# A two-block network on one core: the second head pair's key is taken before its decays, its projections' first terms move to ScalarE, gate slices move, and each attention group's last pair is placed behind a dense tile

## The reference

```python
proj = h @ w_in[l]
att_in, rwkv_in, gate_in = jnp.split(proj, [ATT_IN, ATT_IN + RWKV_IN], axis=-1)
y_att = attention_mixer(att_in) @ w_att_out[l]          # 3 groups x 8 heads of 64, blocks of 128
y_rwkv = rwkv7_mixer(rwkv_in, mu_shift[l], w0[l], ...) @ w_rwkv_out[l]
...
# rwkv7_mixer: z is mixed with the token before, then r, k, v and three low-rank inputs
z = z + (z_prev - z) * mu
w_log = -jax.nn.softplus(-(w0 + jnp.tanh(w_low) @ w2)) - 0.5
decay = jnp.exp(-jnp.exp(w_log))
a = jax.nn.sigmoid(a0 + a_low @ a2)
k_mod = k * (1.0 + (a - 1.0) * k_a)
kk = heads(k * k_k)
kk = kk / jnp.maximum(jnp.sqrt(jnp.sum(kk * kk, axis=-1, keepdims=True)), 1e-12)
# a scan over tokens, 16 heads of 64: state = state*w + (state@(-kk))*(kk*a) + v*k_mod ; y = state@r
bonus = jnp.sum(r_h * k_h * r_k, axis=-1, keepdims=True) * v_h
```

## Time and profile before

| | us |
|---|---|
| median of 3 runs | 2147.8 (2145.29 to 2149.35) |
| the profiled execution, its own time | 2148.11 |
| its span | 2146.1 |
| PE busy | 2053.9 (96%) |
| DVE busy | 1208.1 (56%) |
| POOL busy | 1062.3 (49%) |
| ACT busy | 518.1 (24%) |
| mean granted TensorE clock | 0.979 |

### The profile page before, as it was taken

The page is one execution under the profiler, slowest core; times in us unless marked ns, Lnnn a source line. Parts: engine busy times, 40 slices in busy tenths (PEclk is TensorE's granted clock), DMA queues, the critical chain, the costliest instruction groups (busy, mean ns, idle before and its releaser), DMA issues.

```text
span 2146.1 us, 39153 instructions
## 1 busy us (share of the span) xinstructions
PE 2053.9 (96%) x16093; PEld 1680.8 (78%) x16093; DVE 1208.1 (56%) x1560; ACT 518.1 (24%) x1110; POOL 1062.3 (49%) x776
## 2 busy tenths in 40 slices
PE   8999999899999998999997999999999989999998
PEld 6888787778777787788875877888876868888887
DVE  6888714466667653301178577667772646565423
ACT  2100002333334221303232122232122113232201
POOL 6777664434434464354453033222353665666663
PEclk9999999899999998999998999999999999999999
DMA  4323332253444331221322121112112422223231
GB/s 139 100 89 98 108 98 61 69 163 118 156 124 127 118 98 60 79 75 63 111 54 80 33 63 44 34 55 64 43 51 76 165 97 79 98 98 98 93 102 60
DMA packets 180342, 189.98 MB, mean 89 GB/s; under 512 B 8141, under 2 KB 161372, under 8 KB 179932
## 3 DMA queue, kind: packets, MB, share of 16 engines
q1 hardware_dynamic: 172288, 181.81, 26.6%
q10 hardware_dynamic: 7900, 5.94, 0.9%
HBM read 179.30 MB, written 8.44 MB: 87 GB/s over the span
## 4 chain that ended last, share of the span: by engine, by line
PE 55%; DVE 9%; DVEq 1%; ACT 1%; issue 1%; DMA 1%; ACTq 0%
PE bank L831 8%; PE bank L832 8%; PE bank L833 8%; PE bank L1463 7%; PE bank L1561 2%; PE bank L1424 1%; PE bank L1300 1%; PE bank L1302 1%; PE bank L1301 1%; PE bank L1284 1%; PE bank L1208 1%; PE bank L1209 1%; PE bank L1210 1%; DVE sq L2593 1%; PE bank L966 1%
## 5 line engine op out<-in xcount | busy, mean ns | idle before, releaser
L678 POOL TENSOR_TENSOR wlo<-raws,whi 128x1024 fp32r<-128x1024 f32 (+5 forms) x312 | 675.6, 2165 | 46.5 <-issue 1.5
L676 POOL TENSOR_SCALAR whi<-raws 128x1024 fp32r<-128x1024 f32 (+5 forms) x312 | 333.4, 1069 | 631.7 <-PE bank L1302 259.6
L831 PE MATMUL bank<-hbuf,whi 128*128 128x512 f32 (+2 forms) x840 | 329.1, 392 | 0.0
L833 PE MATMUL bank<-hbuf,wlo 128*128 128x512 f32 (+2 forms) x840 | 327.4, 390 | 0.0
L832 PE MATMUL bank<-hbuf,whi 128*128 128x512 f32 (+2 forms) x776 | 302.6, 390 | 0.0
L628 POOL TENSOR_TENSOR spare<-ones 1x1 f32<-1x1 f32 x92 | 22.5, 244 | 361.8 <-PE bank L833 246.2
L831 PEld LDWEIGHTS bank<-hbuf,whi 128*128 128x128 f32 (+2 forms) x840 | 157.0, 187 | 35.7 <-POOL wlo L678 1.1
L833 PEld LDWEIGHTS bank<-hbuf,wlo 128*128 128x128 f32 (+2 forms) x840 | 157.0, 187 | 34.1
L832 PEld LDWEIGHTS bank<-hbuf,whi 128*128 128x128 f32 (+2 forms) x776 | 145.1, 187 | 31.2
L2488 DVE TENSOR_REDUCE nmax<-bank 128x4 f32<-128x512 f32 (+3 forms) x40 | 21.1, 550 | 151.9 <-PE bank L1183 104.2
L1300 PE MATMUL bank<-hbuf,whi 128*128 128x512 f32 x192 | 84.1, 438 | 0.0
(11 more groups left out here) (482 smaller groups left out, 4612.2 us busy)
## 6 DMA issues: line engine op xcount, KB each, us to landing
adaw<-in_w_ada SPq DMA_DIRECT2D x64, 384.0 KB, 4.0
raws<-in_w_up SPq DMA_DIRECT2D x22, 1024.0 KB, 4.9
raws<-in_w_in SPq DMA_DIRECT2D x41, 512.0 KB, 4.0
raws<-in_w_in SPq DMA_DIRECT2D x18, 1024.0 KB, 5.0
raws<-in_pool_w_in SPq DMA_DIRECT2D x16, 1024.0 KB, 5.3
raws<-in_mla_w_in SPq DMA_DIRECT2D x10, 1024.0 KB, 6.2
raws<-in_pool_w_out SPq DMA_DIRECT2D x8, 1024.0 KB, 4.9
raws<-in_mla_w_out SPq DMA_DIRECT2D x8, 1024.0 KB, 5.2
```

Source lines behind the costliest of these rows:

```text
L676: G.tensor_scalar(h_, r_, 1.0, 1.0, ALU.mult, ALU.mult)
L678: G.tensor_tensor(l_, r_, f32(h_), ALU.subtract).then_inc(raw_split, 1)
L831: M.matmul(dst, wh, acts[k][0], start=(first and k == 0), stop=False)
L833: mm = M.matmul(dst, wl, acts[k][0], start=False, stop=(last and k == n - 1))
```

## The change

Four edits:

1. **Attention.** In the last pair of every group, `following(0)` (24 dense matmuls) stands ahead of both `turned` and of the `values` of the pair before, not between them. The product goes to bank 2 (its sequel to 3), since banks 0 and 1 still hold scores; ACT's query copies and the low-rank products swap banks with it.
2. **Pair 1's key and first terms.** `columns_of(1)` runs at the start. After the bonus product of pair 0, ACT makes the first term (the bank times 1 - mu) of pair 1's k, r and v, with a Copy from PSUM with scale, in place of three DVE TENSOR_SCALARs. DVE takes the key before `log_decays(1)`, and ACT squares it before `decays(1)`. `key_lengths(1)` stays behind the decays.
3. **`bonus_sums(0)`** stands ahead of the last four of the 24 projection slices of pair 1, and ACT copies pair 0's first gate ahead of `decays(0)`.
4. **Gate slices.** Pair 1's 48 gate matmuls stand behind steps 3, 6 and 15 of the first preparation.

```diff
-GATES_BESIDE = {6: (0, 24), 12: (24, 27), 14: (27, 30), 16: (30, 33), 17: (33, 36), 19: (36, 39), 20: (39, 42),
-                21: (42, 45), 23: (45, 48)}
+GATES_BESIDE = {3: (0, 20), 6: (20, 34), 15: (34, 48)}
...
-                        if kind or (g and j):
+                        if kind:
                             two_tiles("att", sg + kind * 2 + j, j, 3 * g + kind, h_out)
+                        elif g and j:
+                            for b in range(2):
+                                bank_free("att", b, 3 * g)
+                                product(bank[b][:, :], 1, 256, b * P, P, h_out, strip=None if b else sg + 1)\
+                                    .then_inc(products_done, 1)
...
                 for t in range(len(units) // 2):
+                    if 2 * t + 2 == len(units):
+                        following(0)
                     turned(2 * t)
                     if t == 0:
                         values_taken((0, 1))
                         scores(2)
                     else:
                         values(t - 1)
-                    if 2 * t + 2 == len(units):
-                        following(0)
                     turned(2 * t + 1)
...
                 rkv(16, 20)
                 if q >= 2:
                     gate(q - 2, q)
+                else:
+                    bonus_sums(0)
                 rkv(20, 24)
                 if q == 1:
-                    bonus_sums(0)
                     key_norms(1)
...
+            def first_term(z, out_):
+
+                product_ready(STRIP0["rkv"] + 3 + z // 2, (1, 0, 1)[z])
+                A.activation(out_[:, :], bank[z][:, :], ACT.Copy, scale=pcol[1][:, 11 + z:12 + z])\
+                    .then_inc(sem(f"rk.first{z}"), 1)
...
             key_squares(0)
             key_lengths(0)
+            take_gate(0, 0)
             decays(0)
-            take_gates(0)
-            wide_part(1)
+            take_gate(0, 1)
+            act.wait_ge(sem("rk.bon"), 1)
+            first_term(1, Kr)
+            sigmoids(1)
+            load_lora(2)
+            act.wait_ge(sem("rk.bs"), 1)
+            first_term(0, Rr)
+            first_term(2, vT[1])
+            key_squares(1)
+            decays(1)
+            key_lengths(1)
             take_gates(1)
...
                 product_ready(STRIP0["rkv"] + q * 3 + z // 2, (1, 0, 1)[z])
-                shifted(bank[z], pc[:, z:z + 1], pc[:, 11 + z:12 + z], out_[:, :]).then_inc(evac[z], 1)
+                if q == 1:
+                    dve.wait_ge(sem(f"rk.first{z}"), 1)
+                    V.scalar_tensor_tensor(out_[:, 1:S], bank[z][:, 0:S - 1], pc[:, z:z + 1], out_[:, 1:S],
+                                           ALU.mult, ALU.add).then_inc(evac[z], 1)
+                else:
+                    shifted(bank[z], pc[:, z:z + 1], pc[:, 11 + z:12 + z], out_[:, :]).then_inc(evac[z], 1)
...
-                if more:
+                if q == 1:
+                    take_key(1)
+                    log_decays(1)
+                elif more:
                     columns_of(q)
                     log_decays(q)
                     take_key(q)
```

More of the change, by code:

```diff
@@ L1244, in following @@
                     if g + 1 < ATT_GROUPS:
-                        bank_free("att", j, 3 * g + 3)
-                        product(bank[j][:, :], 0, 256, j * P, P, h_out, strip=sg + 6 if j == 0 else None)\
+                        bank_free("att", 2 + j, 3 * g + 3)
+                        product(bank[2 + j][:, :], 0, 256, j * P, P, h_out, strip=sg + 6 if j == 0 else None)\
                             .then_inc(products_done, 1)
                     elif j == 0:
-                        bank_free("lora", 0, 0)
-                        product(bank[0][:, :], 0, P, 0, P, h_out, half_at=1, strip=STRIP0["lora"])\
+                        bank_free("lora", 2, 0)
+                        product(bank[2][:, :], 0, P, 0, P, h_out, half_at=1, strip=STRIP0["lora"])\
                             .then_inc(products_done, 1)
                 for t in range(len(units) // 2):
+                    if 2 * t + 2 == len(units):
+                        following(0)
                     turned(2 * t)
@@ L1269, in _ @@
                 units_before += len(units)
-            bank_free("lora", 2, 0)
-            product(bank[2][:, :], 1, 160, 0, P, h_out, strip=STRIP0["lora"] + 1).then_inc(products_done, 1)
+            bank_free("lora", 0, 0)
+            product(bank[0][:, :], 1, 160, 0, P, h_out, strip=STRIP0["lora"] + 1).then_inc(products_done, 1)
             bank_free("lora", 3, 0)
@@ L1905, in _ @@
                         product_ready(sg + kind * 2 + t // 2, t % 2)
-                        o, x = tile(dst, t), bank[t][:, :]
+                        b = (t + 2) % 4 if g and kind == 0 else t
+                        o, x = tile(dst, t), bank[b][:, :]
                         if g:
@@ L1909, in _ @@
                         A.activation(o, x, ACT.Copy, scale=ATT_DIM ** -0.5 if kind == 0 else 1.0)\
-                            .then_inc(evac[t], 1)
+                            .then_inc(evac[b], 1)
                 units = att_units(g)
@@ L1991, in _ @@
                 if pr == 0:
-                    act.wait_ge(evac[0], fill("lora", 0) + 1)
+                    act.wait_ge(evac[2], fill("lora", 2) + 1)
                     A.activation(wlow[0:64, :], wlow[0:64, :], ACT.Tanh).then_inc(sem("lora.act"), 1)
                 if pr == 1:
-                    for b in (2, 3):
+                    for b in (0, 3):
                         act.wait_ge(evac[b], fill("lora", b) + 1)
@@ L2069, in wide_part, with take_gate @@
                     key_lengths(q)
-            def take_gates(q):
-                for turn, j in enumerate(GATE_ORDER[min(q, 1)]):
-                    if turn == 0:
-                        if q < 2:
-                            act.wait_ge(sem("x_kept"), 16)
-                        else:
-                            act.wait_ge(sem("gt.kept"), (q - 1) * 16)
-                    product_ready(STRIP0["rkv"] + q * 3 + 2, turn)
-                    A.copy(tile(xT, q % 2 * 2 + j), gate_dst(q, j)[:, :]).then_inc(sem("gt.taken"), 1)
+            def take_gate(q, turn):
+                j = GATE_ORDER[min(q, 1)][turn]
+                if turn == 0:
+                    if q < 2:
+                        act.wait_ge(sem("x_kept"), 16)
+                    else:
+                        act.wait_ge(sem("gt.kept"), (q - 1) * 16)
+                product_ready(STRIP0["rkv"] + q * 3 + 2, turn)
+                A.copy(tile(xT, q % 2 * 2 + j), gate_dst(q, j)[:, :]).then_inc(sem("gt.taken"), 1)
+            def take_gates(q):
+                take_gate(q, 0)
+                take_gate(q, 1)
+            def first_term(z, out_):
+                product_ready(STRIP0["rkv"] + 3 + z // 2, (1, 0, 1)[z])
+                A.activation(out_[:, :], bank[z][:, :], ACT.Copy, scale=pcol[1][:, 11 + z:12 + z])\
+                    .then_inc(sem(f"rk.first{z}"), 1)
             def chain(p):
@@ L2538, in _ @@
             mu = VEC0["mu_shift_2"]
-            for n, (b, half, out_, rows) in enumerate(((0, (0, 1), wlow[:, :], P), (2, (1, 0), tile(glow, 0), P),
+            for n, (b, half, out_, rows) in enumerate(((2, (0, 1), wlow[:, :], P), (0, (1, 0), tile(glow, 0), P),
                                                        (3, (1, 1), glow[0:32, S:2 * S], 32))):
@@ L2726, in _ @@
             columns_of(0)
+            columns_of(1)
             take_key(0)
```

1 line of the change is left out of this document (added).

## The result

The change is faster by nearly twice what was forecast. The median of four runs is 2128.16 us (2127.84 to 2128.3), that of before, run beside it, 2146.55 us (2144.21 to 2149.35): ratio 0.9922, 95% interval 0.991 to 0.9934, or 18.4 us between the medians where 10.35 were expected. The profiled run of after took 2127.84 us, with a span of 2126.1 us and a mean clock of 0.980.

What follows compares the result with a forecast made beforehand. PE, busy 96% of the span, was taken as the bound, so only its waits and lowered clock counted. Attention 4.15 plus RWKV start 6.2 made 10.35 us off 2147.8: 2137.45, said as 2137.5 (chance 0.55), range 2132.5 to 2142.

Steps and rivals of the forecast that it cites:

- Attention: End of each attention group: PE's three waits for exponentials (1.13, 1.51, 1.51 us) go; gain 4.15 us.
- The statistics: Softmax statistics: first send 4.0 us later, DVE's stretch shrinks from 8 to about 3.2 us, no wait at the combination.
- Rival 2: Softmax statistics arrive late, PE and DVE stand at the combination; gain only 6.1 us, 2141.5 us; chance 0.15.
- rival 3: Nearly nothing left: gates eat the gain, stall 3.8 us, decays end later, statistics late; 2.2 us, 2145.5; chance 0.09.
- rival 4: Slower: the statistics' trip through DRAM gets much longer, ending 14.4 us later; 2152 us and more; chance 0.04.
- Rival 1: More won: no POOL stall of decayed_keys, clock stays before level 6, shorter decays up to 1.5 us; 2133; chance 0.17.
- r out of bank 0 at 1159.5: RWKV start: DVE frees r at 1159.5, so gram A starts then, not at 1166.20: 6.7 us earlier.
- the move of `bonus_sums(0)`: Pair 1's projections: PE waits about 3 us for the bonus product, which costs nothing.
- The first terms: Pair 1's first terms on ACT: one TENSOR_SCALAR (0.8 us) less on DVE's path to r.
- The key ahead of the decays: Pair 1's key: its three operations, 2.1 us, leave DVE's path behind the decays to r.
- The gates: First preparation: 20 gates add 4.7 us ahead of level 0 (1168.0); fewer later, chain starts 1200.1, not 1206.33.
- The stall of `decayed_keys`: Ahead of level 6: POOL's strip split stalls DVE's decayed_keys by 1.5 us, between 0 and 3.8; PE waits 4.0 us.

Runs made afterwards that it cites:

- e1: The kernel before with the attention edit alone: 2139.25 us, ratio 0.9977.
- e7: The change with bonus_sums(0) back at its old place, behind the last projection slices: 2134.91 us, ratio 0.9951.
- e8: e7, with POOL's split of pair 2's first strip held until pair 1's decays are done: 2128.03 us, ratio 0.9919.
- e5: The change once more, nothing altered, run on another occasion: 2128.32 us, ratio 0.9919.
- e2: The change without the attention edit: 2137.48 us, ratio 0.9965.
- e12: The change with the first terms of pair 1's k, r and v made by DVE again: 2127.2 us, ratio 0.9914.
- e15: The change with ACT's squares of the key moved ahead of v's first term: 2127.15 us, ratio 0.991.
- e13: The change with DVE taking pair 1's key behind its decays again: 2135.56 us, ratio 0.9955.
- e9: The change with POOL's splits of pair 2 held, first strip until pair 1's decays, second until decayed_keys(1), are done: 2125.48 us, ratio 0.9902.
- e11: The kernel before with only POOL's split of pair 2's first strip held until pair 1's decays are done: 2142.49 us, ratio 0.9985.
- e10: e9 with the gates split 14, 14 and 20 behind steps 3, 6 and 15: 2123.9 us, ratio 0.9892.
- e14: e10 with the first terms of k, r and v on DVE again: 2122.55 us, ratio 0.9888.

## Why the prediction was wrong

The direction and the order of events were right; the size was not. The times below are put in the frame of before by adding 3.2 us, the difference between the two combinations' starts.

**Attention: right, slightly too small.** All three waits went; from the attention's start to the combination the trace is 4.8 us shorter, 4.15 were predicted, and alone (e1) it is 5.4 us by medians. What is over the sum of the three brackets stays unexplained. The statistics came nearly as told: the first send behind the dense product (1077.50), then 4.1 us of DVE work, where some 3.2 were told, and no wait at the combination. Rivals 2 and 3, which stood on their being late, fell, and rival 4, a much longer trip, with them. Rival 1 pointed the right way and was too small by 5 us: its main reason, no stall in `decayed_keys`, did not come true, and it gave shorter decays 1.5 us at most. (Rival 2's sum gives 2141.7, not 2141.5, which changes nothing.)

**The step that failed: "r out of bank 0 at 1159.5".** It held that `gram A` would wait 5 to 6 us for r and start at 1159.5, with the clock low. It was built on POOL's second strip starting "some 0.5 us later", with the decays 0.8 us earlier. In that frame the decays began at 1151.4, 1.0 later than told, but POOL began at 1153.8 and not near 1151.1. It was released by the last projection, and that came late by the bonus product's own 0.9 us and by what I left out: I priced the move of `bonus_sums(0)` as a wait of 3 us "which costs nothing", and did not let the clock fall behind it. It fell, the bonus matmuls took 2.08 us and not 1.02, and the projections behind them 0.63 us each at first and not 0.40. So POOL missed the scan, the decays took 4.3 us, where I had kept nearly the 8.4 of before, r was out at 1156.9, and `gram A` ran at 1157.1 without a wait. Two consequences: 2.4 us in its start, and about 1.7 us because the grams ran at the upper clock. Level 0 came at 1163.9 where 1168.0 was told. e7 and e8 show it: without the moved sums 6.6 us are lost, and with POOL held nothing is. How much it is varies: in e5, where the clock came back later, level 0 came 1.0 us later behind the bonus sums. The bounds given (1 us later, 2.5 us earlier) held the decays to what a shift of POOL by half a microsecond could do.

**A cost that was a gain.** The move of the bonus sums acted as an unintended hold on POOL. That is a fragile gain: without the attention part (e2) the clock stayed up and POOL met the decays again, though PE waited equally long. Why the clock stayed up there no run shows.

**The first terms: a part with no worth.** The prediction counted 0.8 us for r's TENSOR_SCALAR. e12 has all three back on DVE and is no slower. What they save on DVE is spent in ACT's queue; e15 takes one of its waits away, and the wait only moves on to r.

**The key ahead of the decays: right.** Its price was 2.1 us of DVE; undone, it costs 2.5 to 4.3 us of the length (e13 against e5 and the change), and behind its longer wait the clock is low.

**The gates: right in kind.** From level 0 to the chain the prediction has 32.1 us, the trace 31.4 (e5 32.2). The stall of `decayed_keys` was taken as 1.5 us: it is (e9 removes it and gets 1.5 us back from the wait). The wait before level 6 was told as 4.0 and was 3.84. What the prediction did not see is that the table is worth 6 us only when r is early, and that its 20 gates ahead of level 0 also cover the stall that POOL now gives `inv_U`.

**What is left.** 10.35 us foretold, 4.8 more up to the chain, 0.65 more in the attention make 15.8 of 18.4. By e5's trace it would be 1.9 less. The two spans are 20.0 us apart: the profiled run of after is 1.6 us late where the attention starts, and wins 5.8 us behind the chain's start, in code that is the same. PE of before, in the last preparation:

```profile
1597.92 0.33 PE L1463 MATMUL bank<-inv_D,inv_DA 64*64 64x64 f32 x5 [2.54 <-issue]
...
1615.74 0.73 PE L1463 MATMUL bank<-inv_D,inv_E 64*64 64x64 f32 x17 [2.27 <-issue]
```

PE of after, at the same place:

```profile
1581.73 0.34 PE L1468 MATMUL bank<-inv_D,inv_DA 64*64 64x64 f32 x5 [1.72 <-issue]
```

From the last pair's first low-rank matmul to the last matmul that reads `glow` (the gates' low-rank input) it is 103.4 us before and 98.6 after. But e11 and e1, with the old chain code, have 98.1, and e10, e14 and e15, with the new, 101.7 to 101.9: in twelve traces it is 98.1 to 98.6, in the other five 101.7 and more. So it does not go with the change; e10, e14 and e15 were at their slowest, by 2 to 6 us, in just the run that was profiled. What PE waits for there, no record shows; a share of the spread of before's runs (2140.86 to 2150.26) may be this, which is not shown. How often each kernel falls into it isn't known, and so whether the last 2.6 us are the change's stays open.

**The rule of the Trainium skill** that was weighed ("SBUF — State Buffer", section "Who interferes with whom") is borne out by e7 against e8: the scan, of two SBUF inputs, is held until POOL's subtraction is over, 3.21 us against 1.23, while the operations that read a PSUM bank kept their 0.73 to 0.75 us beside POOL. I had applied it to the new stall in `decayed_keys`, and gave the one that was there and could vanish 0.6 us.

## What to carry to other kernels

Where two engines contend, an edit's value depends on when each meets the other: ask of every wait or clock drop not only who waits for it, but which other engine's background work it releases, and when. If a trace shows an operation at two durations, hold the other engine's work explicitly until it is past (one wait was worth 3 us in the old kernel, two together some 3 in the new), and don't leave it to a side effect. Price an operation that is moved to a less busy engine with the queue that it joins; and price filler work only beside the wait that it fills.

## What the runs showed of the hardware that was not expected

- A wait of the same length took PE's clock along or didn't: 3.29 us in the change, with two bonus matmuls in 2.08 us behind it, and 3.31 us in e2, with 1.12. A wait of 1.30 us left it (1.12 us for the key norms), one of 2.20 took it (e13, 1.58), one of 2.35 left it (e9). The length of a wait alone doesn't tell.
- It also came back at different delays. In e5 and the change the bonus sums began at 1143.62 and 1144.96; the clock was up near 1149.6 and 1148.4, and the last projection ended at nearly the same moment. So a start 1.3 us earlier was lost within 6 us.
- DVE's stall is about as long on a tiny tile as on a large one: 2.15 us for 128x7 (0.17 alone) and 3.21 for the scan of 128x512 (1.23 alone), some 2.0 us in both. POOL is slowed as well: its TENSOR_SCALAR of 128x1024 took 1.95 us beside DVE, 1.04 alone. Two operations that read a single SBUF tile were held too: the copy of `mid` (0.79 us before, 0.17 after) and, in e11, the scaling of `kk` (2.38 us, 0.49 before).
